# A two-layer conv/gMLP encoder step on one core: the last product in parts of 448, 352 and 256 columns, and three small reorderings

## The reference, cut to what matters

```
for l in range(2):
    h = rmsnorm(x, norm_mix[l])
    x = x + (mixer_ab(h) if l == 0 else mixer_c(h))
    h = rmsnorm(x, norm_ffn[l])
    g, up = split(h @ w_up[l]);  x = x + (silu(causal_conv3(g)) * up) @ w_down[l]
y = rmsnorm(x, norm_final)          # x * rsqrt(mean(x*x) + 1e-6) * norm_final
```

## Time and profile before

| what | value |
|---|---|
| median of three runs | 2094.79 us |
| the profiled execution | 2094.42 us |
| its span, first to last instruction | 2092.6 us |
| PE busy | 2080.4 us (99%) |
| DVE, ACT, POOL busy | 1509.2, 747.1, 964.5 us |
| mean granted TensorE clock | 0.999 of full |

### The profile page before, as it was taken

The page is one execution under the profiler, slowest core; times in us unless marked ns, Lnnn a source line. Parts: engine busy times, 40 slices in busy tenths (PEclk is TensorE's granted clock), DMA queues, the critical chain, the costliest instruction groups (busy, mean ns, idle before and its releaser), DMA issues.

```text
span 2092.6 us, 36500 instructions
## 1 busy us (share of the span) xinstructions
PE 2080.4 (99%) x15414; PEld 2072.4 (99%) x15414; DVE 1509.2 (72%) x1843; ACT 747.1 (36%) x1158; POOL 964.5 (46%) x610
## 2 busy tenths in 40 slices
PE   9999999999999999999999999999999999999998
PEld 9999999999999999999999999999999999999998
DVE  6999689766666667666987677798676666766666
ACT  6574354233222322223532223453322233222234
POOL 3867335444443444443565345455444344444344
PEclk9999999999999999999999999999999999999999
DMA  4111211111111110111111111111111111011112
GB/s 167 52 33 68 99 61 42 61 61 41 41 54 49 62 51 31 61 41 61 41 41 62 41 61 41 61 41 61 41 41 61 41 61 51 31 61 42 61 43 89
DMA packets 34036, 115.66 MB, mean 55 GB/s; under 512 B 3985, under 2 KB 6545, under 8 KB 33873
## 3 DMA queue, kind: packets, MB, share of 16 engines
q1 hardware_dynamic: 33728, 112.78, 16.1%
q10 hardware_dynamic: 144, 0.54, 0.1%
HBM read 108.69 MB, written 4.62 MB: 54 GB/s over the span
## 4 chain that ended last, share of the span: by engine, by line
PE 93%; DVE 3%; issue 1%; POOL 1%; ACT 0%; DMA 0%; POOLq 0%; DVEq 0%; ACTq 0%
PE psum L694 31%; PE psum L696 31%; PE psum L695 30%; DVE xs_lo L1969 1%; DVE xs_lo L2209 1%; DVE work L2247 1%; DVE r_rows L2236 1%; POOL x L1378 0%; PE psum L823 0%; DVE work L2249 0%; DVE x L1936 0%; PE psum L766 0%; POOL r_col L1220 0%; DMA raw<-slabs 0%; PE psum L848 0%
## 5 line engine op out<-in xcount | busy, mean ns | idle before, releaser
L694 PE MATMUL psum<-xs_hi,w_hi 128*128 128x264 f32 (+2 forms) x3784 | 1101.5, 291 | 1.1 <-POOL w_lo L1191 0.5
L696 PE MATMUL psum<-xs_hi,w_lo 128*128 128x264 f32 (+2 forms) x3784 | 1100.0, 291 | 0.0
L695 PE MATMUL psum<-xs_lo,w_hi 128*128 128x264 f32 (+2 forms) x3784 | 1096.4, 290 | 0.0
L1191 POOL TENSOR_TENSOR w_lo<-raw,w_hi 128x512 fp32r<-128x512 f32 (+1 forms) x412 | 663.9, 1623 | 822.8 <-ACT w_hi L1417 740.5
L694 PEld LDWEIGHTS psum<-xs_hi,w_hi 128*128 128x128 f32 x3784 | 711.8, 188 | 3.3 <-issue 1.3
L695 PEld LDWEIGHTS psum<-xs_lo,w_hi 128*128 128x128 f32 x3784 | 711.3, 188 | 0.0
L696 PEld LDWEIGHTS psum<-xs_hi,w_lo 128*128 128x128 f32 x3784 | 711.2, 188 | 0.0
L694 PE MATMUL psum<-act_hi,w_hi 128*128 128x352 f32 x1200 | 388.3, 324 | 0.1
L696 PE MATMUL psum<-act_hi,w_lo 128*128 128x352 f32 x1200 | 388.2, 323 | 0.0
L695 PE MATMUL psum<-act_lo,w_hi 128*128 128x352 f32 x1200 | 385.4, 321 | 0.0
L1417 ACT ACTIVATE w_hi<-raw 128x512 fp32r<-128x512 f32 x383 | 234.0, 625 | 289.6 <-PE psum L696 268.8
(11 more groups left out here) (242 smaller groups left out, 1851.0 us busy)
## 6 DMA issues: line engine op xcount, KB each, us to landing
raw<-slabs SPq DMA_DIRECT2D x186, 512.0 KB, 3.3
x<-x_t SPq DMA_DIRECT2D x15, 528.0 KB, 6.0
y_t<-x SPq DMA_DIRECT2D x4, 400.0 KB, 2.9
y_t<-x SPq DMA_DIRECT2D x8, 200.0 KB, 2.1
raw<-slabs SPq DMA_DIRECT2D x4, 256.0 KB, 8.2
y_end<-y_rows SPq DMA_DIRECT2D x4, 256.0 KB, 2.9
x<-x_t ACTq DMA_DIRECT2D x1, 528.0 KB, 4.7
x<-mix SPq DMA_DIRECT2D x1, 512.0 KB, 3.4
```

Of the source, the lines that this page charges most:

```text
L694: nc.tensor.matmul(out, w_hi[:, w], hi, start=start, stop=False, skip_group_check=reopen)
L695: nc.tensor.matmul(out, w_hi[:, w], lo, start=False, stop=False, skip_group_check=reopen)
L696: return nc.tensor.matmul(out, w_lo[:, w], hi, start=False, stop=stop, skip_group_check=reopen)
L1191: nc.gpsimd.tensor_tensor(w_lo[:, slab], src, w_hi[:, slab].bitcast(F32), ALU.subtract).then_inc(weights_ready, 1)
```

## The change

It has four parts.

1. The last product's chunks have 448, 352 and 256 columns in place of 400, 400 and 256. Chunks 0 and 1 are handled in four row tiles of 112 and of 88 frames.
2. In chunk 2 DVE adds up only the squares of tiles 0 to 3. TensorE adds those of tiles 4 to 7 itself: `end_stats` multiplies each by the column of ones into the same PSUM columns. These small products, and the last of them behind the first turned tile, now stand ahead of the turning, which stood ahead of `chunk_stats(2)`. `end_turned` is raised twice, after tiles 0 to 3 (for ACT) and after 4 to 7 (for DVE).
3. Around chunk 1's r: DVE makes its mean square ahead of the first sum of squares of chunk 2, POOL takes it after six of its multiplications in place of seven, TensorE spreads it at tile 5 of chunk 2 in place of tile 6, ACT copies it one tile earlier, DVE's first multiplication of chunk 1 stands right behind tile 4's sum. Chunk 0's r is spread in the middle of tile 4 of chunk 1, in place of ahead of it. The order of the stores and of ACT's scaling follows; there are 17 stores.
4. In the first pair of every stage, `rms_spread` stands behind one half of the first X_B22 product. In stage 1, ACT makes the high part of the first weight entry of that pair ahead of tile 5's scaling instead of behind it.

The core of the diff:

```diff
-FINAL_CUTS = (0, 400, 800, COLS)
+FINAL_CUTS = (0, 448, 800, COLS)
...
-Y_STORES = ((0, 4, 6), (0, 6, KD), (0, 0, 2), (0, 2, 3), (0, 3, 4), (1, 4, 5), (1, 0, 1), (1, 5, 6), (1, 1, 3), (1, 6, 7),
-            (1, 3, 4), ("act", 0), ("act", 1), ("dve", 0), (1, 7, KD), ("dve", 1))
+Y_STORES = ((0, 4, 6), (0, 6, KD), (0, 0, 2), (0, 2, 3), (1, 0, 1), (0, 3, 4), (1, 4, 5), (1, 1, 2), (1, 5, 6), (1, 2, 3),
+            (1, 3, 4), ("act", 0), (1, 6, 7), ("dve", 0), ("act", 1), ("dve", 1), (1, 7, KD))
+END_SUMMED = 4
...
                 pe.wait_ge(part_copied, 3 * n + 3)
+                block_product(a22, X_B22, x_bank, 0, False, False, halves=(0,))
                 rms_spread(p, psum[:, Y_BANK, 300:300 + ROW_REST])
-                for kp in range(KP):
+                block_product(a22, X_B22, x_bank, 0, False, False, halves=(1,))
+                for kp in range(1, KP):
...
+            def end_stats(squares, opens, closes):
+                for t, (at, rows) in enumerate(FINAL_ROWS[2]):
+                    n = 8 + t
+                    last = nc.tensor.matmul(psum[0:rows, 7, n:n + 1], squares[:, at:at + rows],
+                                            one[:], start=opens and t == 0, stop=closes, skip_group_check=True)
+                return last
...
-                    if c and m == (4, 6)[c - 1]:
-                        chunk_spread(c - 1)
+                    if (c, m) == (2, 5):
+                        chunk_spread(1)
...
+            pe.wait_ge(part_summed, KD - 1 + END_SUMMED - 1)
+            end_stats(sumsq, True, False)
+            for m in range(END_SUMMED, KD - 1):
+                pe.wait_ge(square_ready, KD * 6 + m + 1)
+                end_stats(end_square[m], False, False)
+            pe.wait_ge(tile_evacuated, FINAL_EVAC + 2 * KD + 6)
+            end_turn(0)
+            pe.wait_ge(square_ready, KD * 7)
+            end_stats(end_square[KD - 1], False, True).then_inc(stats_ready, 1)
+            for m in (1, 2):
+                end_turn(m)
+            end_turn(3).then_inc(end_turned, 1)
...
             chunk_r(0)
-            chunk_y(0, 7)
+            chunk_y(0, 6)
             chunk_r(1)
-            chunk_y(7, 11)
+            chunk_y(6, 10)
             chunk_r(2)
-            chunk_y(11, len(POOL_Y))
+            chunk_y(10, len(POOL_Y))
...
+                    if p == 1 and m == 5:
+                        entry_hi(p, 0, 0, 0)
                     act.wait_ge(tile_evacuated, read(m))
```

More of the change, by code:

```diff
@@ L91 @@
 SPREAD_STEP = 21
-FINAL_CUTS = (0, 400, 800, COLS)
-FINAL_ROWS = [[(FINAL_CUTS[c] + rows * t, rows) for t in range(n)] for c, (n, rows) in enumerate([(4, 100), (4, 100),
+FINAL_CUTS = (0, 448, 800, COLS)
+FINAL_ROWS = [[(FINAL_CUTS[c] + rows * t, rows) for t in range(n)] for c, (n, rows) in enumerate([(4, 112), (4, 88),
                                                                                                 (2, P)])]
@@ L924, in _, with block_product @@
                 last.then_inc(tile_done, 1)
-            def block_product(slab, which, first_bank, kp, opens, closes, reopen=False):
-                for h in range(2):
+            def block_product(slab, which, first_bank, kp, opens, closes, reopen=False, halves=(0, 1)):
+                for h in halves:
                     at = kp * KP_COLS + which + h * PART
@@ L1127, in chunk_stats, with end_turn @@
                 last.then_inc(stats_ready, 1)
+            def end_stats(squares, opens, closes):
[4 more added lines that the diff above has]
+                return last
+            def end_turn(m):
+                if m < 4:
+                    pe.wait_ge(end_scaled, m + 1)
+                    bank = END_BANKS["act"]
+                else:
+                    bank = END_BANKS["dve"]
+                for t in range(END_ROWS):
+                    last = nc.tensor.transpose(psum[:, bank[t], m % 4 * P:(m % 4 + 1) * P],
+                                               x_t[:, m, END + t * P:END + (t + 1) * P], ident[:])
+                return last
             def chunk_spread(c):
@@ L1161, in _ @@
                     last.then_inc(tile_done, 1)
[L1162 to L1172, removed]
-                                               x_t[:, m, END + t * P:END + (t + 1) * P], ident[:])
-            last.then_inc(end_turned, 1)
-            chunk_stats(2)
+            pe.wait_ge(part_summed, KD - 1 + END_SUMMED - 1)
[10 more added lines that the diff above has]
+            end_turn(3).then_inc(end_turned, 1)
+            pe.wait_ge(tile_evacuated, FINAL_EVAC + 3 * KD)
+            for m in (4, 5, 6):
+                end_turn(m)
+            end_turn(7).then_inc(end_turned, 1)
         @block.gpsimd
@@ L1631, in last_down @@
                         t_high(p, m // 2 - 1)
-                    if m == 5:
+                    if m == 5 and p == 1:
+                        entry_hi(p, 0, 0, 1)
+                    elif m == 5:
                         entry_hi(p, 0, 0, 0, 1)
@@ L2594, in part_squares @@
                 total = psum[:, SUM_BANK, 0:FINAL_CUTS[c + 1] - FINAL_CUTS[c]]
-                dve.tensor_tensor(total if m < KD - 1 else sumsq[:, cols], total, end_square[m][:, cols],
+                dve.tensor_tensor(total if m < (KD if c == 1 else END_SUMMED) - 1 else sumsq[:, cols], total, end_square[m][:, cols],
                                   ALU.add).then_inc(part_summed, 1)
@@ L2613, in _ @@
                     part_squares(1, KD - 1)
-                elif m >= 2:
-                    part_squares(2, m - 1)
-                if m == 2:
+                elif m == 2:
                     chunk_mean_square(1)
-            part_squares(2, KD - 1)
-            chunk_y(1, 0, 1)
+                    part_squares(2, 1)
+                elif m == 4:
+                    part_squares(2, 2)
+                    chunk_y(1, 0, 1)
+                elif m == 5:
+                    part_squares(2, 3)
+            chunk_y(1, 1, 2)
             chunk_mean_square(2)
-            chunk_y(1, 1, 4)
-            dve.wait_ge(end_turned, 1)
+            chunk_y(1, 2, 4)
+            dve.wait_ge(end_turned, 2)
             dve.wait_ge(r_col_ready, 7)
```

15 lines of the change are left out of this document (9 added, 6 removed).

## The result

The changed kernel takes 2098.19 us (median of 20 runs, 2097.51 to 2099.03), the kernel before 2094.47 in the same comparison (2094.05 to 2095.35): ratio 1.0017, 95% interval 1.0011 to 1.0023. The forecast was 2093.0, with a range up to 2095.3. The profiled execution took 2097.74 us, with a span of 2095.9 (before: 2094.42 and 2092.6).

The account below looks back on a forecast made before the run. TensorE, busy 2080.4 of 2092.6 us, was taken to bound the kernel. Spreads -0.66, stage 1 +0.2 and end -1.3 summed to -1.8 us, median 2093.0 us; own range 2092.1 to 2093.9, 8 in 10 range 2090.9 to 2095.3.

Parts of the forecast that it names:

- The spreads: Starts of the three stages: three matmuls ahead of each spread cover TensorE's wait, gain 0.66 us, bounds 0 and 0.96.
- What is late next is r_rows for ACT and DVE: Behind the moved spreads: r_rows up to 0.1 us late, at no cost, as TensorE has the remaining X_B22 product.
- ACT's early high part: Stage 1's start: POOL's earlier w_lo closes TensorE's hole but may block DVE; cost +0.2 us, between -0.1 and +1.4.
- The end: Last product and stores: fewer bytes left and r of chunk 2 earlier, gain 1.3 us, bounds nothing and 2.6.
- POOL's first multiplication: End, after chunk 0's wider columns: starts 0.95 us later, at 2072.0 in place of 2071.07.
- r of chunk 1: End, after six POOL multiplications: ready at 2079.85, where it was 2079.7.
- TensorE's idle time: End, ahead of chunk 1's spread at tile 5: about 0.95 us idle, a cost of 0.6 us.
- Now stats can close about 2083.9: Chunk 2's sums by TensorE close then, giving r at 2084.85 against 2085.18 and output pieces 0.3 us earlier.
- a sign of being wrong: Chunk 2 at the end: the forecast called itself wrong if r of chunk 2 came later than before.
- the DMA's full stretch: Last stores: DMA full for 4.2 instead of 5.4 us, with four y_end pieces and three chunk 1 tiles left.
- D: Rival: stage 1's lock takes the spreads' gain, +1.4 in place of +0.2, total -0.6, 2094.2 us; chance 0.08.
- B: Rival: POOL's slower 448-column multiplications make r of chunk 1 late at the end, 2095.0 to 2095.6 us; chance 0.10.

Follow-up runs that it names:

- e2: Kernel before with only the spread moved inside the first X_B22 product: 2097.24 us, +2.57, ratio 1.0012.
- e4: e2 with DVE's 32-column gate multiply put ahead of the 1024-column one: 2094.24 us, -0.43 against the kernel before.
- e6: Kernel before with only DVE's two gate multiplies exchanged, as control: 2094.46 us, -0.17.
- e3: Kernel before with only ACT's high part of the first weight entry moved ahead in stage 1: 2095.93 us, +1.26.
- e12: e10 without TensorE's sums over the squares of tiles 4, 5 and 6 of the last 256 columns: 2093.63 us, 0.51 under e10.
- e11: e10 with e4's two edits, spread inside the product and short multiply first: 2093.06 us, -1.62 against the kernel before, ratio 0.9993.
- e1: Changed kernel with the spread and ACT's early entry put back, so only the end is changed: 2095.47 us, +0.80 against the kernel before.
- e10: e8 with three filler matmuls of 256 columns ahead of chunk 1's spread: 2094.14 us, -0.54 against the kernel before.
- e5: Changed kernel, whole, with DVE's 32-column multiply ahead of the 1024-column one: 2095.07 us, +0.44 against the kernel before.
- e8: e1 with chunk 1's spread one tile later and DVE's first y behind tile 6's sum: 2094.17 us, -0.46 against the kernel before.
- e13: e10 with DVE summing chunk 2's squares and the blocks turned ahead of the sums, as before the change: 2093.87 us, -0.61 against the kernel before.

## Why the prediction was wrong, point by point

*The spreads, -0.66.* The gain itself was right: 0.78 us came back, between the forecast and the upper bound of 0.96. The step that failed is the sentence behind it: "What is late next is r_rows for ACT and DVE, by up to 0.1 us; [...] so this costs nothing". I asked only what becomes late. What becomes early did the harm: POOL's w_lo comes 0.36 us sooner behind the spread, and that put it ahead of DVE's 32 columns (e2 +2.57, e4 -0.43, e6 no difference). The margin in the kernel before was 0.1 us.

*ACT's early high part, +0.2 with bounds -0.1 and +1.4.* The mechanism and the upper bound were right and the choice was wrong: +1.26 alone (e3). I had written that early w_lo can block DVE once each, then took the row where they meet once. Both met. The argument that r_col and not the hole is on the chain held: in e3 the hole grew by 0.84 us, r_col came 1.15 us later, and 1.15 is what TensorE is late behind the spread.

*The end, -1.3.* It gave 0.17. Four terms came as forecast: POOL's first multiplication 1.02 us later (0.95), r of chunk 1 24.02 us behind the start (24.08), TensorE's idle time of 0.95 us (0.95), 0.85 us from the last byte to the end (0.9). The term that failed is "Now stats can close about 2083.9", that is 28.1 us behind the start, and with it r of chunk 2 "0.3 us earlier". TensorE's last product ended about when it should (26.6 us behind the start, forecast 26.5). The sums began 0.3 us behind it, when DVE's sum of tile 3's squares was through (2086.09), and closed at 29.5. So r is 1.0 us later, which the prediction had named as a sign of being wrong. What I did not price is the 16 matmuls for the sum and tiles 4 to 6 ahead of the closing four, 1.8 us (e12 shows what 12 of them are worth, 0.5 of the tail). The spread that waits for r costs about the 0.6 us that the prediction gave it: moved one tile back, with DVE's first y behind it, the tail is 36.07 us in e11 against 36.66, both at full clock. A smaller miss is the DMA's full stretch, 4.7 us and not 4.2, as four of chunk 1's tiles were still to be stored and not three. The 1.2 us gained behind r and this loss of 1.0 nearly cancel.

*The clock.* That TensorE's clock can fall among these short matmuls, with the blocks still to be turned, was in no rival. It costs about 1.1 us of tail where a profile has it (37.76 in e1 against 36.66 with the same instructions). It would account for e1's +0.80, but e1 has one profile and the clock of its other executions over these few us is not on record. The end at full clock, e2 and e3 add up to -0.17 + 2.57 + 1.26 = 3.66 us, beside 3.72 measured for the whole.

*The rivals.* D had the right mechanism and a third of its price: it saw the lock at the start of stage 1 alone. B put the slower side at the end, at POOL's row, and POOL's multiplications ran in 1.12 us as forecast. No rival asked for the lock behind the spreads. The range ended at 2095.3 because no case in it held the meetings behind the spreads. The misses at the end (1.1) and in stage 1 (1.1) alone would have made 2095.2, inside it. What took the time out of it is the step on the spreads, +2.57 in e2 where -0.66 was forecast.

*What stays open.* Why the clock falls in e10 and not in e11, with the same instructions at the end, and in the changed kernel's profile not at all, no run here tells: the fall comes among or right behind the short matmuls in each of the four profiles that have it (e1, e5, e8, e10), and no more than that is shown. e12 and e13 are e10 with fewer of them and have a full clock, but with one profile each, and e11 has a full clock with all of them. Whether the changed kernel's median (0.45 us above its profiled execution) holds such executions was not seen.

## What to carry to other kernels

Moving an instruction on the bound engine moves everything that its neighbours release. Ask of each release that comes earlier what it will now run beside, and put the short DVE instructions with two SBUF inputs where POOL surely isn't. And leave as little as possible for TensorE behind its last product, since that part may run at half clock, as in four of the profiles here.

## What the runs showed of the hardware

- A DVE multiply of 32 columns took 0.19 us alone and 1.28 us when POOL's w_lo of 512 columns had started 0.13 us ahead of it (changed kernel, stage 3); exchanging it with a multiply of 1024 columns was worth 3.0 us over three places (e2, e4).
- The granted clock fell to 0.50 within the last 5 us of matmuls while TensorE was busy for 3.85 of the 4 us before (e10), and 14 turned blocks took 2.92 to 3.23 us instead of 1.73 (e1, e8, e10).
- A matmul that sums 128 partitions into one column takes 0.12 us, as long as one of 256 columns in the products beside it (changed kernel, from 2084 us on).
